# Latent attention by pairs of heads, its block mask added in VectorE's maximum pass

## The reference

```python
def attend(args):                      # one block of 128 queries; scale = 96 ** -0.5
    qn, qp, blk = args
    s = jnp.einsum("bqhd,bkhd->bhqk", qn, k_nope) + jnp.einsum("bqhd,bkd->bhqk", qp, k_pe)
    s = s.astype(F32) * scale
    q_chunk = (blk * Q_BLOCK + jnp.arange(Q_BLOCK)) // CHUNK      # chunks of 64
    s = jnp.where(key_chunk[None, :] <= q_chunk[:, None], s, NEG_INF)
    p = jax.nn.softmax(s, axis=-1).astype(v.dtype)
    return jnp.einsum("bhqk,bkhd->bqhd", p, v)
```

## Time and profile before

| what | us |
| --- | --- |
| median of 3 runs | 2454.19 |
| lowest, highest run | 2446.77, 2454.20 |
| span of the profiled execution, first to last instruction | 2445.0 |
| latent attention in it, first score product to first product of the output projection | 1064.91 to 1135.36 = 70.45 |
| PE busy in that stage | 56.03 |
| DVE, ACT busy in it | 39.27, 41.34 |
| even layer's attention in it, from one pair's value products to the next pair's | 12.18 |

### The profile page before, as it was taken

One profiled execution on the slowest core, in us unless ns is written; L12 is line 12 of the kernel. 1 busy time (PEld: TensorE's weight loads), 2 busy tenths in 40 slices (PEclk: granted clock), 3 DMA queues, 4 the chain that ended last, 5 costly groups with the idle time before them and its releaser, 6 DMA issues.

```text
span 2445.0 us, 37907 instructions
## 1 busy us (share of the span) xinstructions
PE 2294.9 (94%) x15465; PEld 1950.7 (80%) x15465; DVE 1169.5 (48%) x1545; ACT 943.6 (39%) x1176; POOL 118.6 (5%) x179
## 2 busy tenths in 40 slices
PE   7998899999989888888899999999999998999995
PEld 6864888888877777657777777777789998999995
DVE  3266442323244587553478888888885000001001
ACT  4247332222243354253266767676764000000001
POOL 6011000000000000000000000000000000000000
PEclk9989899999999999999899999999999999999998
DMA  6320223242222000110299999999998877877663
GB/s 192 112 83 1 70 90 101 86 142 78 95 86 65 19 3 3 36 35 1 92 370 351 364 355 359 355 361 355 361 360 298 272 260 235 267 243 259 227 225 114
DMA packets 262116, 451.16 MB, mean 185 GB/s; under 512 B 8359, under 2 KB 148494, under 8 KB 261854
## 3 DMA queue, kind: packets, MB, share of 16 engines
q1 hardware_dynamic: 257216, 435.73, 51.4%
q0 software_dynamic: 4576, 13.41, 2.3%
q10 hardware_dynamic: 190, 0.05, 0.0%
HBM read 436.63 MB, written 12.52 MB: 184 GB/s over the span
## 4 chain that ended last, share of the span: by engine, by line
PE 50%; DVE 2%; ACT 2%; issue 1%; DMA 0%; DVEq 0%; POOLq 0%; SPq 0%; ACTq 0%; POOL 0%
PE bank L694 48%; PE bank L697 2%; DVE w_low L2035 1%; ACT w_high L1953 1%; DVE small L2092 0%; DVE arena L2035 0%; DMA xs<-sum_rows_d 0%; DMA sum_rows_d<-arena,idx_now 0%; DVE arena L2753 0%; ACT arena L1590 0%; DVE arena L2099 0%; ACT xg_high L1959 0%; ACT arena L1582 0%; ACT arena L1968 0%; DVE y_low L2035 0%
## 5 line engine op out<-in xcount | busy, mean ns | idle before, releaser
L2035 DVE TENSOR_TENSOR w_low<-slot,w_high 128x2048 fp32r<-128x2048 f32 x172 | 393.6, 2291 | 331.2 <-ACT w_high L1511 265.6
L694 PE MATMUL bank<-arena 128*128 128x144 f32 (+6 forms) x2672 | 356.9, 298 | 9.2 <-ACT arena L1590 4.5
L694 PEld LDWEIGHTS bank<-arena 128*128 128x128 f32 (+4 forms) x2672 | 316.2, 183 | 25.6 <-issue 11.2
L694 PE MATMUL bank<-arena,slot 128*128 128x144 f32 (+4 forms) x2368 | 309.3, 300 | 9.9 <-issue 5.2
L2035 DVE TENSOR_TENSOR arena<-arena,bank 128x512 f32<-128x512 f32 (+2 forms) x99 | 58.7, 593 | 528.2 <-PE bank L694 528.2
L694 PEld LDWEIGHTS bank<-arena,slot 128*128 128x128 f32 (+2 forms) x2368 | 286.1, 182 | 29.1 <-issue 22.3
L2035 DVE TENSOR_TENSOR w_low<-arena,w_high 128x2048 fp32r<-128x2048 f32 x105 | 239.9, 2289 | 25.7 <-ACT w_high L1953 25.0
L694 PE MATMUL bank<-w_high,xg_high 128*128 128x512 f32 x560 | 227.3, 406 | 6.3 <-DVE w_low L2035 4.2
L1953 ACT ACTIVATE w_high<-slot 128x2048 fp32r<-128x2048 f32 x108 | 206.2, 1915 | 69.5 <-PE bank L694 39.3
L694 PE MATMUL bank<-h_ffn,w_high 128*128 128x512 f32 (+1 forms) x736 | 222.6, 385 | 3.1 <-DVE h_ffn L2035 3.1
L1953 ACT ACTIVATE w_high<-arena 128x2048 fp32r<-128x2048 f32 x105 | 201.1, 1920 | 61.7 <-PE bank L694 61.6
(11 more groups left out here) (368 smaller groups left out, 3321.2 us busy)
## 6 DMA issues: line engine op xcount, KB each, us to landing
slot<-in_moe_w_up_dram SPq DMA_DIRECT2D x86, 1024.0 KB, 6.3
arena<-in_moe_w_gate_dram SPq DMA_DIRECT2D x78, 1024.0 KB, 6.2
arena<-in_moe_w_down_dram SPq DMA_DIRECT2D x64, 1024.0 KB, 5.3
slot<-in_moe_w_down_dram SPq DMA_DIRECT2D x48, 1024.0 KB, 5.4
slot<-in_moe_w_gate_dram SPq DMA_DIRECT2D x34, 1024.0 KB, 5.1
arena<-in_moe_w_up_dram SPq DMA_DIRECT2D x26, 1024.0 KB, 5.6
slot<-in_e_w_in_dram SPq DMA_DIRECT2D x12, 1024.0 KB, 5.8
slot<-in_ff_w_gate_dram SPq DMA_DIRECT2D x11, 1024.0 KB, 5.3
```

Source lines behind the costliest of these rows:

```text
L694: return pe.matmul(o, lhsT, rhs, start=start, stop=True, skip_group_check=True)
L2035: return dve.tensor_tensor(o, a, b, op)
```

## The change

The latent attention takes the even layer's form, with these differences from it:

- the mask is a 128x512 tile `mask_w` in SBUF (zero, and +1e30 in the last 64 columns of the first 64 partitions), written by DVE before the stage. The queries are stored negated (`scale=-MLA_SCALE`), so DVE's minimum of (negated score + mask) is what the exponential needs with scale -1. `chunk_mask`, its two memsets on POOL and 32 products of PE are gone;
- PE, ACT and DVE step by pair rows p = 4 pair + t: six buffers `probs_d`, a ring of six banks;
- four triangular buffers for the transposed probabilities (row k of the keys holds only columns 128k to 511);
- PE's order in a step is scores of p, transposes of p-2, then the value products;
- the value products of a pair alternate between its two heads, so that products to partitions 0 to 63 and 64 to 127 of one bank follow each other;
- `high_odd`, `low_odd`, `high_dense` and `low_dense` stand at other places among the rows.

```diff
+        probs_d, mask_w = region(26256, 6, SEQ), region(29328, SEQ)
+        TRI = SEQ - P
+        probsT_at = (0, NT * TRI + P, 20112, 16400)
+        def probsT_cols(i, t):
+            at = probsT_at[i] + P * t
+            return arena[:, at:at + TRI * (t + 1)].rearrange("p (a b) -> p a b", b=TRI)[:, :, 0:P]
+        def probsT_row(i, k):
+            at = probsT_at[i] + TRI * k
+            return arena[:, at + P * k:at + SEQ]
...
-            link(pool.memset(chunk_mask[:, :], 0.0))
-            link(pool.memset(chunk_mask[0:CHUNK, CHUNK:P], MASKED))
...
+            def latent_attention(first, done):
+                ring = Banks(turn_banks + acc[2:4], None)
+                ring.read = list(turn_bank.read) + [(sem("kpe_ready"), 1)] * 2
+                def pair_tiles(name, p):
+                    for i in (2 * p, 2 * p + 1):
+                        bank[name, first + i + 1], former = ring.open(sem(name), first + i + 1)
                         pe.wait_ge(*former)
+                    return [bank[name, first + 2 * p + hh + 1] for hh in range(2)]
+                for p in range(HEADS // 2 * NT + 3):
+                    if p < HEADS // 2 * NT:
+                        pair, t = divmod(p, NT)
+                        for hh, b in enumerate(pair_tiles("max_ready", p)):
+                            h = 2 * pair + hh
+                            mm(b[:, 0:P * (t + 1)], qT_d[:, h, P * t:P * (t + 1)], kT_d[:, h, 0:P * (t + 1)], True)\
+                                .then_inc(sem("scores_full"), 1)
+                    u = p - 2
+                    if 0 <= u < HEADS // 2 * NT:
+                        pe.wait_ge(sem("probs_scaled"), first + 2 * u + 2)
+                        for hh, b in enumerate(pair_tiles("probsT_ready", u)):
+                            for k in range(u % NT + 1):
+                                m = tp(b[:, P * k:P * (k + 1)], probs_d[:, (2 * u + hh) % 6, P * k:P * (k + 1)])
+                            m.then_inc(sem("probsT_full"), 1)
+                    u = p - 3
                     if u >= 0 and u % NT == NT - 1:
+                        pair = u // NT
+                        pe.wait_ge(sem("probsT_ready"), first + 2 * u + 2)
+                        if pair >= 2:
                             pe.wait_ge(sem("yT_ready"), done + pair - 1)
                         for k in range(NT):
+                            for hh in range(2):
+                                h = 2 * pair + hh
+                                m = mm(acc[pair % 2][64 * hh:64 * hh + 64, P * k:], v_d[:, k, HD * h:HD * (h + 1)],
+                                       probsT_row(2 * (pair % 2) + hh, k), k == 0)
+                        m.then_inc(sem("pv_done"), 2)
+                turn_bank.read[:] = ring.read[0:4]
...
-                def score_d(b, h, t):
-                    mm(b[:, 0:P * (t + 1)], qT_d[:, h, P * t:P * (t + 1)], kT_d[:, h, 0:P * (t + 1)], True)
-                    return mm(b[:, P * t:P * (t + 1)], ident[:, :], chunk_mask[:, :], False)
-
-                attention(HEADS * NT, score_d, lambda h, k: v_d[:, k, HD * h:HD * (h + 1)], 4)
+                latent_attention(HEADS * NT, 4)
...
+            def latent_attention(first, done):
+                for p in range(HEADS // 2 * NT + 4):
+                    if p < HEADS // 2 * NT:
+                        n = P * (p % NT + 1)
+                        for i in (2 * p, 2 * p + 1):
+                            act.wait_ge(sem("max_ready"), first + i + 1)
+                            act.activation(probs_d[:, i % 6, 0:n], probs_d[:, i % 6, 0:n], ACT.Exp, bias=small[:, 48 + i % 4:49 + i % 4], scale=-1.0,
+                                           accum_out=small[:, 52 + i % 4:53 + i % 4]).then_inc(sem("probs_ready"), 1)
+                    u = p - 2
+                    if 0 <= u < HEADS // 2 * NT:
+                        pair, t = divmod(u, NT)
+                        if t == 0 and pair >= 2:
+                            act.wait_ge(sem("pv_done"), 2 * (done + pair - 1))
+                        for hh in range(2):
+                            act.wait_ge(sem("probsT_full"), first + 2 * u + hh + 1)
+                            act.activation(probsT_cols(2 * (pair % 2) + hh, t),
+                                           bank["probsT_ready", first + 2 * u + hh + 1][:, 0:P * (t + 1)].rearrange("p (a b) -> p a b", b=P),
+                                           ACT.Copy).then_inc(sem("probsT_ready"), 1)
+                    if p in (1, 2, 3, 4):
+                        high_odd(p - 1)
+                    if p in (6, 9):
+                        high_dense(phase_splits(O_OUT)[0] + p // 9)
+                    if p % NT == NT - 1 and p >= 7:
+                        pair = p // NT - 1
+                        act.wait_ge(sem("pv_done"), 2 * (done + pair + 1))
+                        act.activation(yT[:, done + pair, :], acc[pair % 2][:, :], ACT.Copy).then_inc(sem("yT_ready"), 1)
                         act.wait_ge(sem("yT_ready"), done + pair + 1)
                         high_odd(done + pair)
...
-                                   ACT.Copy, scale=MLA_SCALE).then_inc(sem("q_stored"), 1)
+                                   ACT.Copy, scale=-MLA_SCALE).then_inc(sem("q_stored"), 1)
...
+            def latent_attention(first, done):
+                for p in range(HEADS // 2 * NT + 1):
+                    if p < HEADS // 2 * NT:
+                        n = P * (p % NT + 1)
+                        for i in (2 * p, 2 * p + 1):
+                            dve.wait_ge(sem("scores_full"), first + i + 1)
+                            if i >= 6:
+                                dve.wait_ge(sem("probsT_full"), first + i - 5)
+                            dve.tensor_tensor_reduce(out=probs_d[:, i % 6, 0:n], in0=bank["max_ready", first + i + 1][:, 0:n], in1=mask_w[:, SEQ - n:],
+                                                     op0=ALU.add, op1=ALU.min, scale=1.0, scalar=-MASKED,
+                                                     accum_out=small[:, 48 + i % 4:49 + i % 4]).then_inc(sem("max_ready"), 1)
+                    u = p - 1
+                    if u >= 0:
+                        n, two = P * (u % NT + 1), 2 * (u % 2)
+                        dve.wait_ge(sem("probs_ready"), first + 2 * u + 2)
+                        step(dve.reciprocal(small[:, 56 + two:58 + two], small[:, 52 + two:54 + two]))
+                        for i in (2 * u, 2 * u + 1):
+                            dve.tensor_scalar(probs_d[:, i % 6, 0:n], probs_d[:, i % 6, 0:n], small[:, 56 + i % 4:57 + i % 4], None,
+                                              ALU.mult).then_inc(sem("probs_scaled"), 1)
+                    if p in (2, 3, 4, 5):
+                        low_odd(p - 2)
+                    if p in (7, 10):
+                        low_dense(phase_splits(O_OUT)[0] + p // 10)
+                    if p in (9, 13):
+                        low_odd(done + p // NT - 2)
+                for k in (2, 3):
+                    low_odd(done + k)
...
+                dve.memset(mask_w, 0.0).then_inc(sem("mask_ready"), 1)
+                dve.wait_ge(sem("mask_ready"), 1)
+                dve.memset(mask_w[0:CHUNK, SEQ - CHUNK:], -MASKED).then_inc(sem("mask_ready"), 1)
+                dve.wait_ge(sem("mask_ready"), 2)
```

76 lines of the change are left out of this document (2 added, 74 removed).

## The result

| | before | after |
|---|---|---|
| median of 4 runs, us | 2454.19 | 2435.22 |
| all runs, us | 2446.77, 2454.19, 2454.20, 2454.24 | 2434.59 to 2436.25 |
| ratio of the times | | 0.9936, 95% interval 0.9921 to 0.9951 |
| span of the profiled execution, us | 2445.0 | 2432.5 |
| latent attention, first score to output projection, us | 70.45 | 50.75 |

The changed kernel is 19.0 us faster by the medians; the forecast was 17.0, at 2437.2. The ratio, which takes in the low run of before, makes it 15.7 (0.0064 of 2454.19).

A forecast was written before the change was run, and what follows sets the result against it. No engine was full; PE held most of the latent attention's chain and waited at hand-overs. Entry 14.5, cycles 12.6 and 11.7, last pair 9.9, tail 4.8 sum to 53.5 against 70.45: 17.0 less, 2437.2 us, range 2426 to 2446.

The forecast's parts named there:

- Entry: Latent attention, first scores to first value products: 14.5 us, between 12.5 and 17.2, corrected from the even layer's 17.17.
- Value products of a pair: Two heads' alternating value products in the latent attention: 2.5 us instead of 3.86, bounds 2.3 and 3.86.
- Settled cycle: One pair of heads in the latent attention: 7.96 + 0.1 + 0.63 = 8.7, plus 2.5 for value products, 11.2 us.
- Last cycle: Last pair of the latent attention: value products 2.5, then 7.4 us behind its 512-key scores, with two overlaps.
- PE in a cycle: PE's own work for a pair in the latent attention: 9.81 + 2 - 1.4 = 10.4 us, fitting closely in the cycle.
- Transposes: Next pair's first-row transposes go ahead of the value products, where PE waits for ACT's copies anyway: -0.36 us a cycle.
- Weight tiles: Side work in the latent attention: `high_dense` on ACT 0; `low_dense` on DVE 1.4 us in the first cycle, 0.5 the second.
- Mask: Mask products on PE in the latent attention: 0.21 us a row, 7 us for 32, not added to the sum.
- rival 3: Value products' 64 weight loads come into the open, 8.7 us in the latent attention; kernel 2445.9 us; chance 0.03.
- Rival 2: PE enters the latent attention at 1.2 GHz, some 4.5 us more; kernel 2441.7 us; chance 0.09.
- Rival 5: PE falls to 1.2 GHz in the latent attention and stays there; kernel slower than before, 2473 us; chance 0.03.
- Rival 6: Same gain, but the changed kernel's median falls on the lower of two values, 7.4 us less: 2429.8; chance 0.12.

The follow-up runs named there:

- the zero products: The changed kernel with 32 added 128x128 PE products behind the scores, identity times a block of zeros; 2436.33 us, ratio 0.9928.
- Moving the side work out: The changed kernel with high parts of outputs, the second weight tile on ACT and the low parts on DVE moved to later rows; 2437.36 us, ratio 0.9933.
- the even layer with both orders: The changed kernel, its even layer's attention also given transposes first and alternating value products; 2428.81 us, ratio 0.9900.
- four banks: The changed kernel with the old ring of four PSUM banks in place of six; 2440.76 us, ratio 0.9954.
- four buffers: The changed kernel with four probability buffers in place of six; 2445.99 us, ratio 0.9973.
- The execution of 3849.59: One execution of the changed kernel with 32 zero products added on PE, at mean granted clock 0.554, left out of its median; 3849.59 us.

## Why the prediction was right, and where it wasn't

**What bounds the kernel.** Fewer hand-overs that PE waits for was the right reading for 13.3 of the 19.7: PE steps aside once in a pair instead of four times. Another 6.0 are less time of PE on the chain, by products that run side by side. Work of PE as such is the smaller thing: the zero products put 8.2 us of it back and cost 1.8 outside the entry, since most of them stand beside ACT's file.

**The template.** Taking the even layer's cycle and correcting it term by term held, each part within 1.2 us:

| | forecast | measured |
|---|---|---|
| entry | 14.5 | 13.30 |
| first cycle | 11.2 + 1.4 | 12.10 |
| second cycle | 11.2 + 0.5 | 11.34 |
| last cycle | 2.5 + 7.4 | 9.36 |
| products and tail | 2.5 + 2.3 | 4.66 |
| stage | 53.5 | 50.75 |

- *Entry.* The term that was mis-sized most, 1.2 too long. I added up to 2.5 for four high parts on ACT and took the middle of a wide bound. By the row of busy time ACT does 12.32 of work in 13.30 there, so little of the high parts can be hidden. My own terms, 17.2 - 2.4 + 2.5 - 4, give 13.3 with the largest correction for the clock, 1.00 against the 0.60 of the earlier trace rows; that it was the clock isn't measured apart.
- *Value products of a pair.* I took 2.5 between 2.3 and 3.86. From the first product (1080.73) to the weights of the 512-key scores behind them it is 2.30, the lower bound: each product of the second head starts 6 ns behind the first head's, and both heads' columns run side by side. The half product of stagger that I added for each step isn't there. Four times 0.2 is 0.8 of the error. The first of the score weights, in the timeline of after:

```profile
1083.03 0.30 PEld L704 LDWEIGHTS bank<-arena 96*128 96x128 f32 x2 [0.17 <-issue]
```

- *Settled cycle.* 8.7 from the 512-key scores to the value products. Moving the side work out showed the bare cycle: 10.42 and 10.49, where my terms without the high part are 11.2 - 0.63 = 10.6.
- *Last cycle.* The six terms of the stretch behind the 512-key scores (1.9, 0.7, 1.0, 1.1, 1.1, 1.3) add up to 7.1, and overlaps should take from that; I wrote 7.4. Measured: 7.06, from 1106.46 to 1113.52.
- *PE in a cycle.* I had 10.4 of work, "closely" fitting. PE was busy for 9.45 and 9.62, so there was more room than I thought.
- *Transposes.* -0.36 for each cycle: put back, they cost 0.07, 0.10 and 0.17. Over-sized here, although the even layer shows it in full.
- *Weight tiles.* I said that `high_dense` costs nothing and `low_dense` 1.4 and 0.5. With both and the high part moved, the cycles lose 1.68 and 0.85, of which I take 0.63 each for the high part, as its own size: 1.05 and 0.2 are left for the tiles. The two weren't moved apart. Right in kind.
- *Mask.* 0.21 a row, confirmed twice: 0.44 for a head of before, and 0.46 and 0.44 in the later cycles of after with zeros put back. My 7 us for 32 rows don't follow from it, since rows that run beside ACT cost next to nothing.

The weight loads, rival 3, stayed hidden. The last pair's sixteen MATMULs in the chain of after, and what follows them:

```profile
1113.52 2.40 PE bank L704 x16
1115.94 0.61 ACT arena L1603
```

Sixteen loads of 0.14 lie in those 2.40, under running products whose weights fill all 128 rows. The page "TensorE: Matmul & The Clock Gate" of the Trainium skill (Part 3: Packing small matmuls — row/col tiling) says that a load overlaps running products only where the row group differs. This trace doesn't agree with that sentence, and the measurement decides; the same section of the Trainium skill also lets a load into a background weight buffer run ahead, and whether that happened here no run shows.

**The clock.** Rival 2 had 0.09. It didn't come in after, but it did in four kernels whose entry has the same or nearly the same code: mean clock 0.89, 0.77, 0.78 and 0.89 for the zero products, the even layer with both orders, four banks and four buffers. The entry then took 14.62 to 15.75 instead of 13.30. Only the kernel with both orders in the even layer has an entry that is the same to the instruction, and its price is 1.3, where I had 4.5; the others hold their own edits as well. Everything that I named for a clock of 1.00 holds for that kernel's entry too, so that after kept it is in part luck. Rival 5, PE stuck at 1.2 GHz, shows in no profile: the longest stretch at half clock inside a latent stage was 10.2 us. The execution of 3849.59 has no profile.

**The base.** The step from the stage to the kernel was right for the wrong reason. I took 17.0 off the median, as if before had two values of equal standing. In 27 runs of before two were near 2447, and the rest at 2451 to 2455.5. Rival 6, with 0.12, rested on the same reading: after's four runs lie within 1.7 us, and no second value showed, which four runs can't exclude. That a stage forecast 2.7 too long and a base that may be off met at 2.0 from the measured time is partly luck. The chances don't follow from their own working either: the cases below 2446.8 come to 0.955, less 0.02 is 0.935, and I wrote 0.90.

**The size.** The stage gave 19.7 instead of 17.0, and the kernel 19.0. That is 2.0 us from the forecast; the interval of the ratio, 2434.8 to 2442.2 us on before's median, holds 2437.2.

## What to carry to other kernels

When a form of the same loop stands elsewhere in the kernel, read its cycle from one row to the next, find the engine whose file has no pause, and correct only what stands on that file: here 8.2 us of work put on PE beside it cost 1.8. Look at what that engine waits for too: a low part of 2.28 on DVE, in front of a pass that ACT waits for, goes with 1.05 of the first cycle. Two 64-wide accumulations that go to different halves of a bank should be issued in turns, product by product, since that costs one exchanged pair of loops and brought 6 us in this stage; in the even layer it was 1.56 of the 1.92 by which a cycle fell. And where PE already waits in an entry, look at its granted clock in more than one execution; a few products that fill the wait may be worth a try, though one matched pair of executions is all that speaks for them here.

## What the runs showed of the hardware

- Two heads' value products (128 rows deep, 64 weights wide, fp32) issued alternately take 2.30 for the pair, and 3.86 one head after the other, with all weight loads hidden in both.
- PE's granted clock isn't fixed by the code of a stretch alone. The same entry took 13.30 at 1.00 when it began at 1062.13 and 14.62 at 0.77 when it began at 1058.57. With seven, four and five products of no use in it and in front of it, it had 1.00 at 1058.65. Without the mask products before's first 10.5 us had 0.59 instead of 1.00, at a start that lay 4.4 later.
- DVE's pass that adds the mask and takes the maximum costs what the maximum alone did, 0.68 to 0.69 for 512 keys, with a read of 0.08 behind it of which all but 0.01 overlaps the pass:

```profile
1097.32 0.68 DVE L2101 CUSTOM_DVE_ANT_0 arena<-bank,arena 128x512 f32<-128x512 f32 x1
1097.93 0.08 DVE L2101 DVE_READ_ACCUMULATOR2_ANT small<- 128x1 f32 x1
```

- A stage that was 2.5 us shorter at full clock left the medians of three kernels where they were, within intervals that are wider than 2.5. Whether something takes it back, and what, wasn't settled.
